# The same program with its SBUF buffers at other addresses: a transformer layer stack on one core

## The reference

```
for l in range(2):                        # first block
    x = x + 0.5 * swiglu(rms_norm(x), w_gate, w_up, w_down)      # 1024 -> 2816 -> 1024
    h = rms_norm(x)
    pa, pb, pc, pd = split(h @ w_in)      # 1024 -> 2464
    # four attention mixers of 256 channels each: neighbourhood, latent, differential, grouped
    x = x + concat(ya, yb, yc, yd) @ w_out
    x = x + 0.5 * swiglu(rms_norm(x), w_gate2, w_up2, w_down2)
    x = rms_norm(x)
h = rms_norm(x); u = h @ w_in_2           # second block, 1024 -> 7424
merged = ga * (ya @ w_proj_a) + gb * (yb @ w_proj_b) + gc * (yc @ w_proj_c)
x = rms_norm(x + merged @ w_out_2)
```

## Time and profile before

| | |
|---|---|
| median of three runs | 1320.54 us |
| profiled execution, its own time | 1319.89 us |
| its span (first to last instruction) | 1317.6 us |
| TensorE busy | 1265.6 us, 96% of the span |
| VectorE busy | 841.5 us, 64% |
| ScalarE busy | 640.0 us, 49% |
| GpSimd busy | 78.7 us, 6% |
| share of the chain that ended last | TensorE 86%, ScalarE 6%, VectorE 5%, DMA 1% |
| DMA engines, mean busy share of the weights' queue | 50.8% |

### The profile page before, as it was taken

One profiled execution on the slowest core, in us unless ns is written; L12 is line 12 of the kernel. 1 busy time (PEld: TensorE's weight loads), 2 busy tenths in 40 slices (PEclk: granted clock), 3 DMA queues, 4 the chain that ended last, 5 costly groups with the idle time before them and its releaser, 6 DMA issues.

```text
span 1317.6 us, 24755 instructions
## 1 busy us (share of the span) xinstructions
PE 1265.6 (96%) x10500; PEld 1239.5 (94%) x10500; DVE 841.5 (64%) x1059; ACT 640.0 (49%) x850; POOL 78.7 (6%) x57
## 2 busy tenths in 40 slices
PE   6999999988999999999999997999999999999997
PEld 6999999978999999999999996899999989899995
DVE  5766677775676666876667686476666754446665
ACT  4433346754543334533335764453333554766542
POOL 1110011210000000000000211000000000000000
PEclk9999999986999999999999995799999999999999
DMA  8876665320565655566665530256655655415542
GB/s 287 219 227 206 191 224 172 114 87 2 182 200 193 191 191 192 170 199 195 194 219 163 166 132 12 65 165 219 192 191 191 200 178 174 128 58 168 176 152 105
DMA packets 169514, 220.33 MB, mean 167 GB/s; under 512 B 5280, under 2 KB 152480, under 8 KB 169312
## 3 DMA queue, kind: packets, MB, share of 16 engines
q1 hardware_dynamic: 165680, 213.66, 50.8%
q0 software_dynamic: 2080, 2.48, 1.0%
q10 hardware_dynamic: 1680, 3.13, 0.7%
HBM read 218.15 MB, written 3.42 MB: 168 GB/s over the span
## 4 chain that ended last, share of the span: by engine, by line
PE 86%; ACT 6%; DVE 5%; issue 1%; DMA 1%; SPq 0%; POOLq 0%; POOL 0%; DVEq 0%; ACTq 0%
PE pj L433 12%; PE pj L437 12%; PE pj L436 12%; PE acc L437 8%; PE acc L436 8%; PE acc L433 8%; PE tr L433 6%; PE tr L437 6%; PE tr L436 6%; PE acc L616 4%; ACT probs L994 2%; ACT w_hi L875 1%; PE tr L608 1%; DVE w_lo L1186 1%; PE tr L586 1%
## 5 line engine op out<-in xcount | busy, mean ns | idle before, releaser
L1186 DVE TENSOR_TENSOR w_lo<-raw,w_hi 128x2048 fp32r<-128x2048 f32 (+2 forms) x206 | 459.4, 2230 | 241.7 <-ACT w_hi L875 240.3
L875 ACT ACTIVATE w_hi<-raw 128x2048 fp32r<-128x2048 f32 (+2 forms) x206 | 381.2, 1854 | 395.3 <-PE pj L433 142.0
L433 PE MATMUL pj<-hT_hi,w_hi 128*128 128x256 f32 x992 | 277.2, 279 | 3.0 <-DVE w_lo L1186 2.4
L437 PE MATMUL pj<-hT_hi,w_lo 128*128 128x256 f32 x992 | 275.8, 278 | 0.0
L436 PE MATMUL pj<-hT_lo,w_hi 128*128 128x256 f32 x992 | 275.7, 278 | 0.0
L437 PE MATMUL acc<-act_hi,w_lo 128*128 128x256 f32 x704 | 194.3, 276 | 0.0
L433 PE MATMUL acc<-act_hi,w_hi 128*128 128x256 f32 x704 | 194.3, 276 | 0.0
L436 PE MATMUL acc<-act_lo,w_hi 128*128 128x256 f32 x704 | 194.3, 276 | 0.0
L433 PEld LDWEIGHTS pj<-hT_hi,w_hi 128*128 128x128 f32 x992 | 187.5, 189 | 4.5 <-DVE w_lo L1186 2.6
L436 PEld LDWEIGHTS pj<-hT_lo,w_hi 128*128 128x128 f32 x992 | 187.3, 189 | 0.0
L437 PEld LDWEIGHTS pj<-hT_hi,w_lo 128*128 128x128 f32 x992 | 187.1, 189 | 0.0
(11 more groups left out here) (212 smaller groups left out, 1989.6 us busy)
## 6 DMA issues: line engine op xcount, KB each, us to landing
raw<-in_w_in SPq DMA_DIRECT2D x47, 1024.0 KB, 5.3
raw<-in_ffn_w_up SPq DMA_DIRECT2D x44, 1024.0 KB, 5.3
raw<-in_ffn_w_down SPq DMA_DIRECT2D x44, 1024.0 KB, 5.0
raw<-in_ffn_w_gate SPq DMA_DIRECT2D x43, 1024.0 KB, 5.4
raw<-in_w_out SPq DMA_DIRECT2D x12, 1024.0 KB, 4.9
raw<-in_w_proj_a SPq DMA_DIRECT2D x4, 512.0 KB, 3.5
raw<-in_w_proj_b SPq DMA_DIRECT2D x4, 512.0 KB, 3.9
raw<-in_w_proj_c SPq DMA_DIRECT2D x4, 512.0 KB, 3.4
```

Source lines behind the costliest of these rows:

```text
L433: ins = pe.matmul(out, lhs[0], rhs[0], start=first, stop=False, **kw)
L437: return pe.matmul(out, lhs[1], rhs[0], start=False, stop=last, **kw)
L875: act.activation(w_hi[r % RING][:, 0:w], raw[r % RING][:, 0:w], ACT.Copy).then_inc(hi_set, 1)
L1186: dve.tensor_tensor(w_lo[r % RING][:, 0:w], raw[r % RING][:, 0:w], w_hi[r % RING][:, 0:w].bitcast(F32), ALU.subtract).then_inc(lo_set, 1)
```

## The change

Only the order of the allocations is changed, and one unused buffer of 96 bytes (`pad`) is added. No instruction is added, removed or moved: on each engine the sequence of instructions of the changed kernel is the sequence of before, and the loads have the same sizes and the same order. What differs is the SBUF address that each operand has. From the two built programs, in bytes from the start of a partition:

| buffer | before | after | before modulo 2048 | after modulo 2048 |
|---|---|---|---|---|
| xT, hn, hT_hi, hT_lo | 4224 to 36991 | 6144 to 38911 | 128 | 0 |
| act_hi, act_lo | 36992, 41088 | 38912, 43008 | 128 | 0 |
| raw (three) | 141248, 149440, 157632 | 47104, 55296, 63488 | 1984 | 0 |
| w_hi (three) | 165824, 174016, 182208 | 71680, 79872, 88064 | 1984 | 0 |
| w_lo (three) | 190400, 198592, 206784 | 96256, 104448, 112640 | 1984 | 0 |
| up_buf, qkT, probs, probsT, bias_buf, scratch, pooledT | 64896 to 128383 | 120832 to 184319 | 1408 | 0 |
| diag, r_row | 137152, 139200 | 184320, 186368 | 1984 | 0 |
| proj | 45184 | 188416 | 128 | 0 |
| const | 131616 | 208128 | 544 | 1280 |
| row | 128384 | 212480 | 1408 | 1536 |
| stat | 135968 | 4352 | 800 | 256 |
| ones | 136480 | 4736 | 1312 | 640 |

Before, every large buffer but `const` starts at a multiple of 64 bytes; `const`, `stat` and `ones` start 32 bytes past one. The diff:

```diff
+        half = sb("half", [P, 32])
+        stat = sb("stat", [P, 96])
+        ones = sb("ones", [P, P])
+        gain2 = sb("gain2", [P, L, DC])
+        smx = sb("smx", [P, 2, 4])
+        ssum = sb("ssum", [P, 2, 4])
+        sinkx = sb("sinkx", [P, 2, 4])
+        lam = sb("lam", [P, 4])
+        xr = sb("xr", [P, 4])
+        cols_buf = sb("cols", [P, L + 1, NCOL])
+        pad = sb("pad", [P, 24])
         xT = sb("xT", [P, DC, S])
         hn = sb("hn", [P, T, D])
         hT_hi = sb("hT_hi", [P, DC, S], F32R)
         hT_lo = sb("hT_lo", [P, DC, S], F32R)
         act_hi = sb("act_hi", [P, 2, 2, S], F32R)
         act_lo = sb("act_lo", [P, 2, 2, S], F32R)
-        proj = sb("proj", [P, T, PW])
+        raw = [sb(f"raw{i}", [P, SLOT]) for i in range(RING)]
+        w_hi = [sb(f"w_hi{i}", [P, SLOT], F32R) for i in range(RING)]
+        w_lo = [sb(f"w_lo{i}", [P, SLOT], F32R) for i in range(RING)]
         up_buf = sb("up_buf", [P, 2048])
...
         pooledT = sb("pooledT", [P, 4, S])
-        row = sb("row", [P, NROW])
-        cols_buf = sb("cols", [P, L + 1, NCOL])
-        gain2 = sb("gain2", [P, L, DC])
-        const = sb("const", [P, NCONST])
-        stat = sb("stat", [P, 96])
-        half = sb("half", [P, 32])
-        ones = sb("ones", [P, P])
...
         diag = sb("diag", [P, 4, P])
         r_row = sb("r_row", [P, 2, S])
-        raw = [sb(f"raw{i}", [P, SLOT]) for i in range(RING)]
-        w_hi = [sb(f"w_hi{i}", [P, SLOT], F32R) for i in range(RING)]
-        w_lo = [sb(f"w_lo{i}", [P, SLOT], F32R) for i in range(RING)]
+        proj = sb("proj", [P, T, PW])
+        const = sb("const", [P, NCONST])
+        row = sb("row", [P, NROW])
```

## The result

The changed kernel is slower: 1364.7 us in the median of four runs (1363.19 to 1370.44), against 1320.66 us for the kernel before in the same comparison. The ratio is 1.035, with a 95% interval from 1.031 to 1.039. The forecast was 1319.9 us, so it was wrong by 45 us.

What follows compares the result with a forecast made beforehand. The prediction took TensorE to bound the kernel, busy for 96% of the span, mostly with float32r matmuls at 113.3 ns. All its terms were zero, giving 1319.9 us (no change, 0.79), range 1307 to 1329 us.

Steps and rivals of the forecast that it cites:

- Float32r matmuls: 9,024 × 0 ns: TensorE's float32r matmuls keep 113.3 ns each, so no change; bounds 27 us upwards and 60 us downwards.
- rival (b): TensorE reads slower, both operands starting at multiples of 2048: feed-forward slots 5.66 us, +27 us, 1347 us; chance 0.07.
- the upper level of before: Slower of two matmul spacings in the trace, 117.8 against 113.3 ns; upward bound in the feed-forward parts, 27 us.
- The first compared operands that had changed roles: Feed-forward slots and token projections show the same two levels, so the level doesn't go with the moving operand or its start.
- The second said that the starts step: Within a slot weights step by 512 or 1024 bytes, so a clash would come and go, yet the distance stays the same.
- the 6.6 ns that the clock didn't explain: Part of each full-speed float32r matmul above 106.7 ns for 256 columns; at most 60 us to return by better placement.
- Traffic into the rings: DMA loads into the weight rings don't slow TensorE, so the rings' place beside the activations has nothing to relieve.
- VectorE, ScalarE, plain float32 matmuls and the transposes against `ident`: Terms taken as 0: the two engines are hidden behind TensorE; the some 600 plain instructions give under 1 us.
- The chain at the start: The uncovered first load of 8.41 us could shrink or grow by 3.0 us; taken as 0.
- Rival (c): Loads get quicker, the start shortens by up to 3.0 us, 1317 us; chance 0.10, counted as no change.
- Rival (d): Granted clock falls otherwise, mostly in the mixing; 1.5 us between layers, three or four times that crosses half a per cent; chance 0.07.
- Rival (a): TensorE reads faster: 1260 us in full, 1307 us if only the upper level outside the feed-forward parts vanished; chance 0.08.

Runs made afterwards that it cites:

- e8: Changed kernel with `raw` alone at 1856 bytes past a multiple of 2048: 1365.66 us in one run.
- e1: Changed kernel's buffer order, with gaps putting every large buffer back to its remainder modulo 2048 of the kernel before: 1326.43 us, ratio 1.007.
- e3: Changed kernel with all large buffers moved up together by 128 bytes, distances between them unchanged: 1366.97 us in one run.
- e16: Changed kernel with all `w_hi` at 64 and `w_lo` at 192 past a multiple of 256, activations and `raw` at 0: 1317.90 us, ratio 0.9987.
- e7: Changed kernel with `w_hi` alone at 1856 bytes past a multiple of 2048: 1347.58 us in one run.
- e17: Kernel before with one gap of 128 bytes between `w_hi` and `w_lo`: 1318.13 us, ratio 0.9988.
- e4: Changed kernel with ring buffers 0, 1 and 2 at 64, 128 and 256 bytes past a multiple of 2048: 1356.59 us in one run.
- e5: Changed kernel with ring buffers 0, 1 and 2 at 192, 384 and 448 bytes past a multiple of 2048: 1349.08 us in one run.

## Why the prediction was wrong

**The term that failed** is "Float32r matmuls: 9,024 × 0 ns". It is +6.67 ns in the 6,144 feed-forward matmuls, 41 us. The mechanism was rival (b), with a chance of 0.07: equal starts (equal modulo 256, as the runs show) slow TensorE's reads, and it decides in the feed-forward slots. Its price, 27 us, was too low, since I took the upper level of before as the worst case. A third level, 120.0 ns, wasn't in the trace. The count of 9,024 was short as well, by 468 float32r matmuls: 336 in the first slots of a stage (lines 477, 480 and 485), 96 of 512 columns in the last product and 36 of 384 or 512 columns in the mixing. That changes nothing in the 6,144.

**Two arguments led there, and both had the same hole.** The first compared operands that had changed roles and found the same two levels. But weights and activations changing roles turns a distance of 1856 into one of 192 modulo 2048, that is 64 into 192 modulo 256. These are two of eight classes, and the table has the same two levels, 113.3 and 117.8 ns, for both. The rows compared two classes that behave alike; they didn't show that the distance is without effect. The second said that the starts step by 512 or 1024 bytes within a slot, so that a clash would come and go. With a period of 256 bytes every one of these steps is zero. The argument excluded only clashes whose period doesn't divide 512, and I used it against all of them.

**The hint that was in the trace** was the 6.6 ns that the clock didn't explain, and above all that they were gone at 1.2 GHz. (The profile gives a granted clock of 1.00 for the stretch of rows 7; the spacing there is that of 18.11 to 20.88, where it gives 0.50.) I counted them as a possible gain. They can be read as a cost that TensorE's reads already paid, and what is paid partly can be paid more fully: the changed kernel's 120.0 ns are 13.3 ns over the 106.7 ns of the columns, twice the 6.6, and they too are gone at 1.2 GHz (213.8 ns). That reading isn't shown for the 6.6 ns themselves, since no layout with 256 columns went below 113.3 ns.

**What held.** Traffic into the rings doesn't slow TensorE by where it goes (e8, and e1 for the place). VectorE, ScalarE, plain float32 matmuls and the transposes against `ident` cost nothing. The chain at the start became shorter by 0.48 us, inside the 3.0 us. Rival (c): the loads land 0.3 us sooner with destinations at multiples of 256, and it isn't only the slower pace of TensorE that does it: e3, as slow but with `raw` 128 bytes past such a multiple, has 5.4 us, and e16, as fast as before but with `raw` at one, has 5.2. It isn't clean either, since e8, with `raw` 64 bytes past, has 5.2 too. The rule that the Trainium skill gives in "DMA: Bandwidth & Descriptors", section "How a descriptor splits into AXI transactions", by which a descriptor that starts off a multiple of 256 bytes takes more transactions, agrees in sign. A fifth off the time it isn't: 5.1 against 5.4 us is 6%. It was hidden, as forecast. Rival (d) was priced too low: not 1.5 us but 5.9 us lie between the two layers in e7, at mean granted clocks of 0.91 and 0.87. Rival (a), TensorE reading faster, came true only for the 512-column matmuls, 0.16 us a slot in four slots.

**The spread** of the kernel before, which I put down to the clock, is probably in part the choice of a level for each feed-forward part. One part at the upper level costs 1,536 × 4.4 ns = 6.8 us, and the layout in whose parts only the lower level was seen (e16, e17) has no execution above 1320.7 us but the one of 2054.79. The kernel before took from 1307.95 to 1335.95 us over all comparisons, apart from the one of 2525.41. None of its long executions has a trace, so this is inferred; e1, with the same remainders, does show one part at the upper level.

**Open:** which reads of the three matmuls meet at what moment, and what sets the level at distance 64. That TensorE reads SBUF in some unit that repeats every 256 bytes is inferred from the table, not shown directly, and one kind of slot (e4 against e5) speaks against it; distances that aren't multiples of 32 weren't tried.

## What to carry to other kernels

When two operands of TensorE are read at full rate in float32r, look at the difference of their starts modulo 256 bytes before laying buffers out on a round grid: round starts for all is the case where they are equal, and it was 6% slower for each matmul of 256 columns. With 512 columns moving it was 3% faster, so measure the shape that carries the time. When a trace offers an argument that a variable has no effect, write down which values of it the rows contain, modulo every period that could matter. A unit cost above its floor is a sign that something is being paid, and a change can make it pay more as well as less.

## What was unexpected of the hardware

- Spacing of 256-column float32r matmuls at the full clock: from 113.3 over 116.7, 117.2, 117.8, 118.3, 118.7, 119.5 and 120.0 to 120.7 ns, by the starts of the operands alone. At a granted clock of 0.50 the kernel before and the changed one had 213.1 and 213.8 ns, with nothing above the columns' time.
- At one layout two levels, 113.3 and 117.8 ns, each held for a whole feed-forward part (1,536 matmuls). With `w_hi` at 64 and `w_lo` at 192 modulo 256 ahead of the activations only the lower one was seen there (two profiles).
- 512-column matmuls with moving weights go the other way: 226.7 ns at equal starts, 233.3 ns before.
- 160-column float32r matmuls took 111.7 ns in both layouts, nearly as much as 256 columns.
- Plain float32 matmuls of 64 columns kept 108 ns in the layout of before and in the changed one.
